# Shorter first stage and router chain, and overflow columns in pairs of chunks, in a two-layer hybrid trunk with top-2 experts

## The reference

```python
def pooling_mixer(h, w_pool, scale):      # 4 groups of channels, trailing windows 2/4/8/16
    ...
    y = jnp.einsum('bsgc,gcd->bsgd', p, w_pool).reshape(B, S, D)
    return y * scale

def moe_swiglu(h, w_router, w_gate, w_up, w_down):
    logits = jnp.dot(t, w_router, preferred_element_type=jnp.float32)
    top_val, top_idx = lax.top_k(logits, TOP_K)          # 2 of 8
    gates = jax.nn.softmax(top_val, axis=-1)
    ...
    for e in range(N_EXPERTS):
        out = out + combine[:, e:e + 1] * swiglu(t, w_gate[e], w_up[e], w_down[e])
```

## Time and profile before

| | us |
|---|---|
| median of 3 runs | 1209.94 |
| lowest, highest | 1209.86, 1210.7 |
| the profiled execution | 1209.54 |
| span in its profile | 1207.8 |
| PE busy | 1176.4 (97%) |
| DVE busy | 196.5 |
| ACT busy | 127.2 |
| POOL busy | 16.7 |
| mean granted TensorE clock | 0.990 |

### The profile page before, as it was taken

The page is one execution under the profiler, slowest core; times in us unless marked ns, Lnnn a source line. Parts: engine busy times, 40 slices in busy tenths (PEclk is TensorE's granted clock), DMA queues, the critical chain, the costliest instruction groups (busy, mean ns, idle before and its releaser), DMA issues.

```text
span 1207.8 us, 15302 instructions
## 1 busy us (share of the span) xinstructions
PE 1176.4 (97%) x6611; PEld 564.5 (47%) x6612; DVE 196.5 (16%) x393; ACT 127.2 (11%) x276; POOL 16.7 (1%) x54
## 2 busy tenths in 40 slices
PE   7999999999999999999999999999999999999996
PEld 5655988874465333334334233433423433343342
DVE  2642000000042210110112011011102101110112
ACT  1342000000021110000011000010100001110002
POOL 1300000000000000000000000000000000000000
PEclk9999999999998999999999999999999999999998
DMA  8425044536563997999999999999999999999991
GB/s 322 168 105 206 3 174 187 237 142 288 212 258 139 366 380 303 397 431 428 433 428 430 427 426 427 434 426 427 433 430 419 432 426 433 429 430 426 429 402 49
DMA packets 18614, 402.93 MB, mean 334 GB/s; under 512 B 3136, under 2 KB 3168, under 8 KB 3936
## 3 DMA queue, kind: packets, MB, share of 16 engines
q1 hardware_dynamic: 18528, 401.67, 79.2%
HBM read 400.61 MB, written 1.05 MB: 333 GB/s over the span
## 4 chain that ended last, share of the span: by engine, by line
PE 96%; DVE 2%; ACT 1%; DMA 1%; issue 0%; SPq 0%; DVEq 0%; ACTq 0%
PE bank L1209 32%; PE bank L1281 16%; PE bank L1075 12%; PE bank L1221 8%; PE bank L1109 6%; PE bank L1294 5%; PE bank L1179 3%; PE bank L980 2%; PE bank L1035 2%; PE bank L1188 1%; PE bank L1252 1%; PE bank L1193 1%; PE bank L964 1%; DMA ring<-attn_w_qkv 1%; PE bank L969 1%; PE bank L994 1%
## 5 line engine op out<-in xcount | busy, mean ns | idle before, releaser
L1209 PE MATMUL bank<-ring,arena 128*64 128x448 f32 x2048 | 394.4, 541 | 0.0
L1209 PEld LDWEIGHTS bank<-ring,arena 128*64 128x64 f32 x2048 | 143.5, 137 | 249.2 <-issue 249.1
L1281 PE MATMUL bank<-ring,arena 128*64 128x512 f32 x896 | 196.7, 594 | 0.0
L1075 PE MATMUL bank<-ring 128*128 128x256 f32 (+1 forms) x768 | 152.8, 362 | 0.0
L1075 PEld LDWEIGHTS bank<-ring 128*128 128x128 f32 x768 | 136.0, 190 | 17.0 <-issue 0.5
L1281 PEld LDWEIGHTS bank<-ring,arena 128*64 128x64 f32 x896 | 62.6, 137 | 127.9 <-issue 127.9
L1221 PE MATMUL bank<-ring,arena 128*32 128x448 f32 x1024 | 102.8, 542 | 0.0
L1109 PE MATMUL bank<-ring,arena 128*128 128x512 f32 x176 | 75.7, 592 | 0.0
L1221 PEld LDWEIGHTS bank<-ring,arena 128*32 128x32 f32 x1024 | 30.0, 109 | 69.8 <-issue 69.8
L857 DVE TENSOR_TENSOR arena<-bank,arena 128x448 f32<-128x448 f32 x32 | 20.0, 625 | 254.2 <-PE bank L1209 254.2
L1294 PE MATMUL bank<-ring,arena 128*32 128x512 f32 x448 | 58.0, 596 | 0.0
(11 more groups left out here) (154 smaller groups left out, 512.3 us busy)
## 6 DMA issues: line engine op xcount, KB each, us to landing
ring<-moe_w_gate SPq DMA_DIRECT2D x32, 3584.0 KB, 19.1
ring<-moe_w_up SPq DMA_DIRECT2D x32, 3584.0 KB, 21.2
ring<-moe_w_down SPq DMA_DIRECT2D x32, 3584.0 KB, 25.3
ring<-attn_w_qkv SPq DMA_DIRECT2D x3, 2048.0 KB, 13.6
ring<-ffn_w_gate SPq DMA_DIRECT2D x2, 3072.0 KB, 10.7
ring<-ffn_w_up SPq DMA_DIRECT2D x2, 3072.0 KB, 10.6
ring<-ffn_w_down SPq DMA_DIRECT2D x2, 3072.0 KB, 14.1
ring<-ffn_w_gate SPq DMA_DIRECT2D x2, 2560.0 KB, 13.5
```

What stands on the lines that cost most here:

```text
L1075: last = mm(bank[u % 4][:, half * S + ts.start:half * S + ts.stop], w[:, k, f:f + P], hT[:, k, ts], start=k == 0, stop=k == KD - 1)
L1209: last = mm(bank[2 * (j % 2) + up][64 * h:64 * h + 64, 0:FJ], xg[:, k, 0:BASE], w[:, k, h, :], start=k == 0, stop=k == KD - 1)
L1281: last = mm(bank[2][64 * h:64 * h + 64, :], hg[:, i0 + i, half * BASE:half * BASE + BASE], w[:, i, h * BANK:h * BANK + BANK], start=d == 0 ...
```

## The change

Four parts.

1. **First stage.** The four gain vectors come in one transfer, laid out by the host. The first chunk comes in halves, and SP waits for it before it issues more. TensorE transposes `ident` 26 times while it waits for data. It then computes the values of tile 0 by halves of the chunk, the keys, and the values of tile 1.
2. **Router chain.** The gains go into the router's weights, and the logits are taken from x without the norm (a factor per token doesn't change which are largest; the difference of the top two is multiplied by `rstd`). TensorE transposes `xres` itself, ScalarE copies the result to `rT`. Each half of a map has a semaphore of its own and is added on its own. 14 more transposes of `ident` (`keep_busy`) stand in the chain. On DVE the flags are computed ahead of the gates.
3. **Gate and up.** Both bases come first, then the overflow of both chunks.
4. **Down.** Base, base, then the overflow of both chunks, 14 tiles in one go.

```diff
             sp.dma_start(xres[:, 0, :], xt[0]).then_inc(x_in[0], 16)
-            for i, g in enumerate((attn_norm, ffn_norm, pool_norm, moe_norm)):
-                sp.dma_start(gain_rows[KD * i:KD * i + KD, :],
-                             g[0].rearrange("(k p) -> k p", p=P)).then_inc(rows_in, 16)
+            sp.dma_start(gains[:, :], norm_gains).then_inc(gains_in, 16)
             sp.dma_start(xres[:, 1, :], xt[1]).then_inc(x_in[1], 16)
+            kv, kv_src = stream[C_QKV]
+            sp.dma_start(kv[:, 0:KD // 2, :], kv_src[:, 0:KD // 2, :]).then_inc(kv_half, 16)
+            sp.dma_start(kv[:, KD // 2:KD, :], kv_src[:, KD // 2:KD, :]).then_inc(full[0], 16)
+            sp.wait_ge(full[0], 16)
...
-            for q in (2, 3):
-                for t in range(T):
-                    norm(q, t)
+            for t in range(T):
+                norm(2, t)
+            for t in range(T):
+                norm(3, t)
+                for kh in range(2):
+                    act.wait_ge(tr_done, 4 * T + 2 * t + kh + 1)
+                    nc.scalar.activation(rT[:, 4 * kh:4 * kh + 4, t * P:t * P + P],
+                                         bank[2 * t + kh][:, :].rearrange("p (k s) -> p k s", k=4),
+                                         ACT.Copy).then_inc(rT_ready, 1)
...
+            gained(router[:, :, :], router[:, :, :], 3 * KD, KD).then_inc(router_ready, 1)
...
+            def add_mix(t, h):
+                dve.wait_ge(mix_done if h else mixh_done, t + 1)
+                xs = xres[:, t, h * BANK:h * BANK + BANK]
+                if h:
+                    dve.wait_ge(xh_ready, t + 1)
+                nc.vector.tensor_tensor(xs, bank[4 + 2 * t + h][:, :], xs,
+                                        ALU.add).then_inc(x_ready if h else xh_ready, 1)
+
+            add_mix(0, 0)
+            add_mix(0, 1)
+            add_mix(1, 0)
             norm(3, 0)
-            add_x(1, 4, mix_done, 2)
-            keep_hT(0, 3 * KD, 0, 4 * T, rT)
+            add_mix(1, 1)
             norm(3, 1)
-            keep_hT(1, 3 * KD, 0, 4 * T, rT)
...
             pe.wait_ge(ident_ready, 1)
-            pe.wait_ge(rows_in, 64)
-            nc.tensor.transpose(bank[7][:, 0:4 * KD], gain_rows[:, :],
-                                ident[0:4 * KD, 0:4 * KD]).then_inc(gains_T, 1)
+            for _ in range(26):
+                nc.tensor.transpose(bank[7][:, 0:P], ident[:, :], ident[:, :])
             transposes(0, 0)
...
+            def keep_busy(n):
+
+                for _ in range(n):
+                    nc.tensor.transpose(bank[7][:, 0:P], ident[:, :], ident[:, :])
...
-            for t in range(T):
-                transposes(3, 0, (t,))
-                pe.wait_ge(hT_ready, 4 * T + 2 * t + 2)
+            map_groups(0, 0)
+            map_groups(0, 1)
+            map_groups(1, 0)
+            pe.wait_ge(poolT_ready, 2 * T)
+            raw_transposes(0)
+            map_groups(1, 1)
+            pe.wait_ge(router_ready, 1)
+            pe.wait_ge(const_ready, 1)
+            logits(0)
+            raw_transposes(1)
+            keep_busy(4)
+            logits(1)
...
                     last.then_inc(up_done if up else gate_done, 1)
-                    with pe.If(ext > 0):
-
+                    with pe.If(ext < 1):
+                        pe.sem_inc(upx_done if up else gatex_done, 1)
+                    with pe.Else():
+                        pass
+
+                with pe.If(ext > 0):
+                    for up in range(2):
+                        w = ring[moe_slot(2 * j + up)][:, :].rearrange("p (k h c) -> p k h c", k=KD, h=2)
                         if j >= 1:
                             pe.wait_ge(upx_ready if up else gatex_ready, 4 * it + j)
...
+                    if d % 2 == 0:
+                        continue
+
                     with pe.If(ext > 0):
-
                         pe.wait_ge(hgxA_ready, it + 1)
                         pe.wait_ge(hgxV_ready, it + 1)
-                        for i in range(ID):
-                            ii = i0 + i
+                        for ii in range(NI):
+                            w = cols(moe_slot(c - 1 + ii // ID), ID, D)
...
+                            if ii % ID == ID - 1:
+                                last.then_inc(downx_done, 1)
```

More of the change, by code:

```diff
@@ L142, in trunk_kernel @@
         iota_i = part(ring[5], 6656, 2 * P).bitcast(I32)
-        gain_rows = ring[5][0:4 * KD, 6912:6912 + P]
         aT = part(arena, 0, NFT, S)
@@ L344, in load_chunk @@
                 sp.dma_start(ring[s][:, :], w.rearrange("o p n -> (o p) n")).then_inc(full[s], 16)
-            for n, (dst, src) in enumerate(stream):
+            for n, (dst, src) in list(enumerate(stream))[1:]:
                 if n == 2:
@@ L643, in _ @@
             norm(0, 1)
-            dve.wait_ge(gains_T, 1)
-            nc.vector.tensor_copy(gains[:, :], bank[7][:, 0:4 * KD]).then_inc(gains_ready, 1)
-            dve.wait_ge(gains_ready, 1)
+            dve.wait_ge(gains_in, 16)
             for t in range(T):
@@ L834, in _ @@
             keep_xg(1)
+            dve.wait_ge(egate_ready, 1)
+            own.link(nc.vector.tensor_scalar(gate2[:, :, 2], gate2[:, :, 1], 1.0, None, ALU.add))
+            own.link(nc.vector.reciprocal(gate2[:, :, 2], gate2[:, :, 2]))
+            own.link(nc.vector.tensor_tensor(gate2[:, :, 3], gate2[:, :, 1], gate2[:, :, 2], ALU.mult))
+            for t in range(T):
+                own.link(nc.vector.tensor_scalar(comb[:, t, 0:NE], pick[:, t, 0, :], gate2[:, t, 2:3],
+                                                 None, ALU.mult))
+                own.link(nc.vector.scalar_tensor_tensor(
+                    out=comb[:, t, 0:NE], in0=pick[:, t, 1, :], scalar=gate2[:, t, 3:4],
+                    in1=comb[:, t, 0:NE], op0=ALU.mult, op1=ALU.add))
+            for r in range(1, ROUNDS):
+                own.step(nc.vector.tensor_copy(comb[:, :, r * NE:r * NE + NE], comb[:, :, 0:NE]))
+                own.step(nc.vector.tensor_scalar(slot[:, :, r * NE:r * NE + NE], slot[:, :, 0:NE],
+                                                 float(CAP * r), None, ALU.subtract))
+            own.wait()
             dve.wait_ge(flags_ready, 1)
@@ L953, in _, with values_of @@
             pe.wait_ge(ident_ready, 1)
-            pe.wait_ge(rows_in, 64)
-            nc.tensor.transpose(bank[7][:, 0:4 * KD], gain_rows[:, :],
-                                ident[0:4 * KD, 0:4 * KD]).then_inc(gains_T, 1)
+            for _ in range(26):
+                nc.tensor.transpose(bank[7][:, 0:P], ident[:, :], ident[:, :])
             transposes(0, 0)
+            w = stream[C_QKV][0]
+            def values_of(t, ks):
+                for k in ks:
+                    last = mm(bank[7][:, t * KVW:t * KVW + KVW], hT[:, k, t * P:t * P + P],
+                              w[:, k, KVW:2 * KVW], start=k == 0, stop=k == KD - 1)
+                return last
+            pe.wait_ge(kv_half, 16)
+            pe.wait_ge(hT_ready, 2)
+            values_of(0, range(KD // 2))
+            chunk_landed(C_QKV)
+            values_of(0, range(KD // 2, KD))
             pe.wait_ge(hT_ready, 2 * T)
-            pe.wait_ge(gains_ready, 1)
-            chunk_landed(C_QKV)
-            w = stream[C_QKV][0]
             for m in range(2):
@@ L966, in _ @@
             last.then_inc(qkv_done, 1)
-            for t in range(T):
-                for k in range(KD):
-                    last = mm(bank[1][:, t * KVW:t * KVW + KVW], hT[:, k, t * P:t * P + P],
-                              w[:, k, KVW:2 * KVW], start=k == 0, stop=k == KD - 1)
-            last.then_inc(qkv_done, 1)
+            values_of(1, range(KD)).then_inc(qkv_done, 1)
             def queries(m, pairs=range(4)):
@@ L1223, in gate_up @@
                         last.then_inc(upx_done if up else gatex_done, 1)
-                    with pe.Else():
-                        pe.sem_inc(upx_done if up else gatex_done, 1)
+                with pe.Else():
+                    pass
             def flag(at):
@@ L1285, in expert @@
                     last.then_inc(down_done, 1)
+                    with pe.If(ext < 1):
+                        pe.sem_inc(downx_done, 1)
+                    with pe.Else():
+                        pass
+                    if d % 2 == 0:
+                        continue
                     with pe.If(ext > 0):
```

95 lines of the change are left out of this document (45 added, 50 removed).

## The result

The changed kernel takes 1199.06 us (median of 6 runs, 1195.95 to 1200.95) against 1209.9 before (6 runs, 1208.93 to 1210.76): a ratio of 0.9908 with a 95% interval of 0.9893 to 0.9922. The forecast was 1194, range 1189 to 1201: faster, but by 10.4 in the profiled execution (1199.1 against 1209.54) where the sum said 15.2. The six runs carry mean granted clocks of 0.990 to 0.993.

What follows compares the result with a forecast made beforehand. TensorE, busy 97% of the span, was taken to set the time, with the transfers 8.4 us behind. Gains of 5.4 (first stage), 3.8 (router) and 6.0 (experts) sum to 15.2, from 1209.54 to 1194, range 1189 to 1201.

Steps and rivals of the forecast that it cites:

- the forecast's own: Whole kernel: the forecast proper, 1194 us with its own range 1191 to 1197, was given 53%.
- rival 3: Experts: waits for weight chunks lower TensorE's clock, costing up to 6 us where the last two are caught: 1200; 15%.
- First stage: Start to the queries: earlier data and warm transposes start the queries at 23.4 instead of 28.8, gain 5.4 (2.8 to 5.6).
- Router: Router chain to experts' start: gain 3.8, with the clock falling once more just ahead of the gather; ends 2.6 and 6.3.
- rival 1: Router chain: the clock holds through it, gaining 6.3 instead of 3.8, total 1191.5; 18%.
- TensorE's saving: Experts: the paired order saves TensorE 3.1 us in each of four experts with overflow, 12.4 in all.
- What of it reaches the end: Experts: transfers cap TensorE's saving; landings 2.4 later and a last-chunk lead of 8.4 let 6.0 arrive (4 to 8.4).
- The tail: Behind the last down projection: the forecast put no change here, 0.
- rival 5: Plain experts: jumps over 64 matmuls (56 in down) in 24 places outrun queued instructions and stall TensorE, making it slower; 4%.

Runs made afterwards that it cites:

- best_a: Changed kernel with the gains' transfer issued third, gate and up paired in every overflow expert, down paired in the 7th expert alone: 1193.02 us.
- best_b: Changed kernel with the gains' transfer third, gate and up paired in every overflow expert, down paired only in the 5th and 7th: 1191.6 us.
- pair_late: Changed kernel with the old order (base, overflow, base, overflow) in the first expert alone, the other three overflow experts still paired: 1195.65 us.
- gains_mid: Changed kernel with the gains' transfer issued third, behind both x tiles and ahead of the first chunk's halves: 1197.05 us.
- gains_last: Changed kernel with the gains' transfer issued fifth, behind both halves of the first weight chunk: 1200.77 us, one run.
- no_warm: Changed kernel with one warm transpose in place of the first stage's 26: 1201.18 us, one run.
- gu_only: Changed kernel with pairs in gate and up only; down takes base and overflow chunk by chunk as before: 1194.96 us.
- down_only: Changed kernel with pairs in down only; gate and up take base and overflow chunk by chunk as before: 1197.34 us.
- pair_off: Changed kernel with the old order (base, overflow, base, overflow) in all experts; first stage and router chain stay changed: 1200.7 us.

## Why the prediction was right or wrong

The time lies inside the stated range and outside the forecast's own, 1191 to 1197. What took it there are two terms that came out smaller (3.3 for 5.4 and 3.6 for 6.0) and one that was put at nothing (0.7). The 3.6 lies below the 4 given as that term's lower end. The room up to 1201 had been kept for rival 3, together with a first stage of 2.8 and frees that are late in further experts; its lower clock cost nothing in the change, and the frees were later in the first expert. That the room covered these errors is in part luck.

**First stage, 5.4 forecast, 3.3 measured: a size.** The step that failed is "The four copies to hT [...] then run from about 8.3, and two of them are done at 9.6", with its premise that the 1.24 of idling in the earlier trace rows "goes when x comes earlier". The copies run from 10.0. x's second tile is issued 0.94 sooner and lands 0.63 later or more (7.61; before, 6.98 at most), since the gains' 128 pieces go out ahead of it; put behind it, they free 2.0 us, and the queries start at 23.70 (24.21 and 24.34 in best_a and best_b). The premise was worth 1.1 to 1.8 of the 2.1 that were missed. The chunk's halves land at 10.07 and 12.53, not at 8.7 and 11.1; with the gains third it is 8.8 and 11.3 (9.4 and 11.8 in best_a), so the gains account for half of this or more. Right: 64 matmuls at the rate of L969, and the next chunk hidden. That the first 32 ran "partly at 1.2 GHz" before was read from their 9.52; the granted clock reads 1.00 there.

**Router, 3.8 forecast, 4.2 measured: right, the clock's place included.** It fell once more, just ahead of the gather, as taken. The upper end (6.3, rival 1) is right too: in three of the twelve profiles of changed kernels (pair_late, gains_mid, gains_last) the clock held, and from the queries to the experts the first two took 338.0 and 338.3, which is 6.6 and 6.4 less than before (the third 336.6, behind queries that came late). Rival 1 is not excluded by the design; it is what happens in some executions.

**TensorE's saving, 12.4 forecast, 13.5 measured: right.** Gate and up give 4.6 in all (forecast 0.9 an expert, 3.6), so down 8.9 for its four, 2.2 each (2.2).

**What of it reaches the end, 6.0 forecast, 3.6 measured: the mechanism right, two readings wrong.** The first is "Both travel together: 489.8 + 11.5 + 8.6 = 509.9, which is 2.4 later". Chunk 4 was issued at 482.5, as the sum has it (489.8 less the 7.5 by which the experts start sooner), but with chunk 3 still in flight until 466.7 + 18.2 = 484.9, so the 11.5 of an empty queue became 13.7. Chunk 5 lands at 504.7, which is 138.8 from the start of the experts against 507.5 - 373.48 = 134.0: 4.8 later, twice the 2.4. I had followed the frees of the second pair and not those of the first, which was late by 5 as well (issued 98.3 after the start of the experts, against 93.4 before).

The second is "TensorE can't start on the last chunk before it is there, so of 12.4 only 8.4 - 2.4 = 6.0 arrives". The cap is not at the last chunk, whose lead I had measured because it was the last. It is at the 7th expert's second chunk, which a pair needs directly behind the first base. Two views of the kernel before show it: the chain, and that chunk's transfer.

```profile
998.42 6.16 PE bank L1209 x32
```

```profile
L344 SPq DMA_DIRECT2D ring<-moe_w_up x1: 333/333/333, 958.7 to 958.7; - x1
...
DMA to landing us min/median/max: 32.1/32.1/32.1
```

It landed at 990.8, 617.3 after the start of the experts, with 7.6 to spare. After, it lands at 987.2, 621.3 after that start, and TensorE waits for it: 7.6 - 4.0 = 3.6, the measured gain to the tenth. From this base to the end both kernels take 196.1 (1194.49 - 998.42, and 1183.31 - 987.26). pair_late (in its profile more gain with more work for TensorE, with the first expert in the old order) and best_a and best_b (the gain arrives when down's pairs come only where the lead allows) bear both readings out.

**The tail, nothing forecast, 0.7 lost.** The gap ahead of the last scatter is 1.47 to 1.79 in the eight kernels whose last expert goes through the paired form of down, and 0.58 to 0.80 in the five that don't (the table's last column). That form makes TensorE jump over 56 matmuls at once, in place of 28 twice, where nothing is left to cover it. The transfers of instructions fit: in the 9 us ahead of this scatter the eight kernels have three blocks of 16 KB on the queue q8, the five have two, and in all thirteen the last block moves 0.25 to 0.75 before the scatter starts (in slices of 0.25). So TensorE seems to wait there for its own instructions. That would be rival 5's mechanism, at 0.9 and in the one exposed place; in the other 23 a plain expert still runs at 24.20. It is not shown: no run takes the jump away alone.

**Rival 3** (waits lower the clock) came true in part: at the 5th expert the base behind a wait took 7.93 instead of 6.2. There it cost nothing, since the next wait was for the transfers again. In gains_mid, gains_last, no_warm and pair_late it fell at the 7th expert, behind the last wait, where the base takes 7.81 to 7.93 instead of 6.23, and there it costs: in gains_mid and gains_last, whose chunk lands as late as the change's, the experts take 1.5 to 1.8 more. By the Trainium skill, "TensorE: Matmul & The Clock Gate", section "HAM oscillation — how this bites in real kernels", a kernel that waits for a transfer before each group is throttled at every one; in the change four waits brought one fall.

## What to carry to other kernels

When two resources are within 1% of each other, work out the lead of every transfer and not of the last one, and look for the smallest where the new order asks for a chunk sooner than the old one did. An order that saves work and frees buffers in pairs can lose more by late frees than it wins (here in the first expert): take it where the lead is widest, and keep the old order where the queue runs dry. Among the first transfers, put the ones with the smallest pieces behind those that the first computation waits for, but not behind the large ones. Where the runs of one kernel lie some us apart, compare them at like granted clock before a difference of medians is given a cause.

## What the runs showed of the hardware that I had not expected

- A 16 KB transfer in 128 pieces of 128 B delayed a 512 KB transfer issued behind it by 2.0 us (landing 7.61 against 5.64): 0.5 is the issue of the small one, 1.5 is time in flight (5.9 against 4.4), where its bytes at 427 GB/s are 0.04. The Trainium skill, "DMA: Bandwidth & Descriptors", section "Specifications", names 512 B as the least transfer for the full rate; the rows agree in direction (before, in 32 pieces of 512 B, 4.3 in flight for the tile).
- The granted clock falls in different places in executions of like code. In gu_only, down_only and gains_last it fell to 1.2 GHz at the first value matmuls, from 11 or 12 us on, behind a stretch in which TensorE idled; in the first two it was back by 15 us and the queries came 1.5 and 1.7 later. In the change it stayed at 2.4, behind a like stretch. These are gu_only's window and chain there (3.69 in the change for the same 16 matmuls):

```profile
11.00:15.00 4.00, 3.81 (x11) 3.06 (x11) 1.35 (x3) 0.00 (x0) 0.00 (x0) 0.57 0.54 143
```

```profile
11.30 5.30 PE bank L975 x16
```

- Falls at the first values (1.5), in the router (2.1) and behind a late chunk (1.7) are each as large as a term of the sum, and come or not by the execution. One profile can't size a term of 2 us in such a kernel, and neither can medians of few runs: the mean granted clock of pair_off's runs goes from 0.992 to 0.998, and their times from 1204.08 to 1197.77.
